# Rotary halves copied by ScalarE, parameters copied earlier, and a first query product that waits tile by tile

## What is computed

```python
mod = adaln(c, w_mod[l], b_mod[l])[:, None, :]          # silu(cond) @ w_mod + b_mod
mod_c = adaln(c_ctx[None, :], w_mod[l], b_mod[l])[:, None, :]
h = modulate(rmsnorm(x, p['g_pre_mix']), sh1, sc1)       # 1024 tokens
h_c = modulate(rmsnorm(ctx, p['g_pre_mix']), sh1c, sc1c) # 256 context tokens
...
def apply_rope(x, cos, sin):
    half = DIFF_HEAD // 2                                # 32
    x1, x2 = x[..., :half], x[..., half:]
    return jnp.concatenate([x1 * cos - x2 * sin, x1 * sin + x2 * cos], axis=-1)
```

## Time and profile before

| | |
|---|---|
| time, median of 3 runs | 3546.27 us (3546.17 to 3559.31) |
| time of the profiled execution | 3547.34 us |
| its span | 3545.4 us |
| mean granted TensorE clock | 0.977 |
| TensorE busy (matmul) | 3366.9 us, 95% |
| VectorE busy | 1923.6 us, 54% |
| ScalarE busy | 907.9 us, 26% |
| opening, until the first query product | 0 to 58.5 us |
| heads, until the last copy | 58.5 to 268 us |

### The profile page before, as it was taken

One profiled execution on the slowest core, in us unless ns is written; L12 is line 12 of the kernel. 1 busy time (PEld: TensorE's weight loads), 2 busy tenths in 40 slices (PEclk: granted clock), 3 DMA queues, 4 the chain that ended last, 5 costly groups with the idle time before them and its releaser, 6 DMA issues.

```text
span 3545.4 us, 57659 instructions
## 1 busy us (share of the span) xinstructions
PE 3366.9 (95%) x25645; PEld 2093.7 (59%) x25645; DVE 1923.6 (54%) x3171; ACT 907.9 (26%) x1850; POOL 51.2 (1%) x117
## 2 busy tenths in 40 slices
PE   6998879998999999889999999999999999999998
PEld 3445655558888888444444444445566447777753
DVE  2036763537676676655555550126988775444524
ACT  3005651115454554221010000100111413233310
POOL 2000000000000000000000000000000000000000
PEclk9999999999999999999999999999999999999999
DMA  6001002310000000331111112113011121100021
GB/s 242 0 0 56 1 24 72 120 58 3 18 18 4 4 4 17 115 113 65 48 59 48 45 60 80 43 59 98 24 36 36 62 76 54 36 24 24 1 89 65
DMA packets 110715, 177.24 MB, mean 50 GB/s; under 512 B 5443, under 2 KB 66626, under 8 KB 109826
## 3 DMA queue, kind: packets, MB, share of 16 engines
q1 hardware_dynamic: 101682, 144.67, 12.1%
q10 hardware_dynamic: 8784, 28.89, 2.3%
HBM read 147.33 MB, written 26.21 MB: 49 GB/s over the span
## 4 chain that ended last, share of the span: by engine, by line
PE 83%; DVE 9%; ACT 4%; DMA 2%; issue 1%; POOL 0%; ACTq 0%; DVEq 0%; SPq 0%; POOLq 0%
PE psum_all L66 82%; ACT sbuf_all L72 3%; DVE sbuf_all L91 3%; DVE sbuf_all L99 2%; DVE sbuf_all L81 2%; PE psum_all L111 1%; ACT L72 1%; DMA sbuf_all<-in_x 1%; DVE sbuf_all L105 1%; DVE sbuf_all L88 0%; DMA sbuf_all<-in_w_out 0%; DMA sbuf_all<-in_w_up 0%; DVE sbuf_all L111 0%; POOL sbuf_all L81 0%; DMA yd_spill<-sbuf_all 0%
## 5 line engine op out<-in xcount | busy, mean ns | idle before, releaser
L66 PE MATMUL psum_all<-sbuf_all 64*64 64x64 f32 (+8 forms) x24890 | 3270.0, 318 | 135.0 <-ACT sbuf_all L72 60.7
L66 PEld LDWEIGHTS psum_all<-sbuf_all 64*64 64x64 f32 (+3 forms) x24890 | 2010.7, 155 | 1370.7 <-issue 980.2
L72 ACT ACTIVATE sbuf_all<-psum_all 128x256 f32<-128x256 f32 (+6 forms) x889 | 363.9, 427 | 1457.6 <-PE psum_all L66 1316.7
L91 DVE SCALAR_TENSOR_TENSOR sbuf_all<-sbuf_all 128x520 f32<-128x520 f32 (+8 forms) x783 | 581.0, 776 | 16.9
L81 DVE TENSOR_TENSOR sbuf_all<-sbuf_all 128x640 f32<-128x640 f32 (+11 forms) x543 | 450.6, 853 | 134.2 <-ACT sbuf_all L72 91.3
L72 ACT ACTIVATE sbuf_all<-sbuf_all 128x64 f32<-128x64 f32 (+12 forms) x475 | 266.5, 574 | 821.5 <-DVE sbuf_all L75 349.1
L75 DVE COPY sbuf_all<-psum_all 128x256 f32<-128x256 f32 (+6 forms) x141 | 72.5, 524 | 473.4 <-PE psum_all L66 448.3
L72 ACT ACTIVATE sbuf_all<-psum_all,sbuf_all 128x1280 f32<-128x1280 f32 (+5 forms) x212 | 164.4, 781 | 313.5 <-PE psum_all L66 275.2
L81 DVE TENSOR_TENSOR sbuf_all<-sbuf_all,psum_all 128x512 f32<-128x512 f32 (+2 forms) x160 | 102.0, 639 | 250.6 <-PE psum_all L66 249.3
L105 DVE COPY_PREDICATED sbuf_all<-sbuf_all,psum_all 128x256 f32<-128x256 int32 (+2 forms) x296 | 144.0, 490 | 69.7 <-PE psum_all L66 64.1
L87 DVE TENSOR_SCALAR sbuf_all<-sbuf_all 128x256 f32<-128x256 f32 (+9 forms) x151 | 57.4, 417 | 162.6 <-ACT sbuf_all L72 159.4
(11 more groups left out here) (21 smaller groups left out, 167.6 us busy)
## 6 DMA issues: line engine op xcount, KB each, us to landing
sbuf_all<-in_w_mod SPq DMA_DIRECT2D x12, 2048.0 KB, 7.9
sbuf_all<-in_w_up SPq DMA_DIRECT2D x22, 1024.0 KB, 7.6
sbuf_all<-in_w_in SPq DMA_DIRECT2D x6, 2048.0 KB, 9.5
x_spill<-sbuf_all SPq DMA_DIRECT2D x16, 512.0 KB, 2.8
sbuf_all<-in_conv_w_in SPq DMA_DIRECT2D x16, 512.0 KB, 5.2
sbuf_all<-in_gla_w_in SPq DMA_DIRECT2D x8, 1024.0 KB, 5.3
sbuf_all<-in_w_down SPq DMA_DIRECT2D x4, 1792.0 KB, 7.5
hid_spill<-sbuf_all ACTq DMA_DIRECT2D x9, 512.0 KB, 2.6
```

Of the source, the lines that this page charges most:

```text
L66: return self.e.matmul(out, lhsT, rhs, start=start, stop=stop, skip_group_check=True)
L72: return self.e.activation(out, in_, func, bias=bias, scale=scale, **kw)
L91: return self.e.scalar_tensor_tensor(out, a, s, b, op0, op1) if self.e is not None else Unissued()
```

## The change

Three edits. The halves of the rotary embedding are swapped by ScalarE: for each half piece four activations of 32 partitions x 512 columns, two of them with scale -1, from the piece into `K.rot` at partitions shifted by 32; the 16 matmuls, their PSUM banks and the matrix `turn` go, and VectorE reads `K.rot` where it read PSUM. VectorE and ScalarE now work on the first four pieces during the key products and on the other four during the value products. The transposes and copies of parameter groups 1 to 6 stand ahead of modulation block 3 on TensorE and VectorE. And the first norm does the token columns of each tile before its context columns, while TensorE waits for one tile at a time in its query products and for the whole of the first norm only ahead of the key products.

```diff
@@ opening_scalar, and the same in opening_vector
-        for a, b, scale, shift in ((0, CTX, K.gs1c, K.modc), (CTX, ALL, K.gs1, K.mod)):
+        for a, b, scale, shift in ((CTX, ALL, K.gs1, K.mod), (0, CTX, K.gs1c, K.modc)):
             x = K.hT[:, j, a:b]
-            se.activation(x, x, ACT.Identity, ...).then_inc(*O.s.tick())
+            se.activation(x, x, ACT.Identity, ...).then_inc(*O.s.tick("first_norm", j, a))
@@ opening_vector
     turned(2)
+    for g in range(1, len(K.groups)):
+        params(g)
     modulation(3)
     mod_turned(3)
...
-    for g in range(1, len(K.groups)):
-        params(g)
@@ heads_tensor
-    te.wait_ge(*K.opening.v.by("first_norm"))
-    te.wait_ge(*K.opening.s.final())
     te.wait_ge(*K.opening.g.final())
+    def rows(k, a, b):
+        te.wait_ge(*(K.opening.s if k % 2 else K.opening.v).by("first_norm", k, CTX))
+        return hT[:, k, CTX + a:CTX + b]
     w = open_block(K, te, ("q",), 512)
...
-            product(te, bank, lambda k: w[:, k, j * P:(j + 1) * P], lambda k: hT[:, k, CTX + a:CTX + b],
+            product(te, bank, lambda k: w[:, k, j * P:(j + 1) * P], lambda k: rows(k, a, b),
                     KD).then_inc(*H.t.tick("q", j, s))
     K.weights.end(("q",), H.t.now())
+    for e in (K.opening.v, K.opening.s):
+        te.wait_ge(*e.final())
     w = open_block(K, te, ("k",), 512)
...
-        if i == 0:
-            te.wait_ge(*H.s.by("qk"))
-            te.wait_ge(*H.v.by("qk"))
-            te.wait_ge(*K.dma("rope").final())
-        if i < len(ROPES):
-            for half in range(2):
-                x, _, _ = rope_views(K, i, half)
-                bank = open_bank(K, te, "rope", i, half)
-                te.matmul(bank, K.turn, x).then_inc(*H.t.tick("rope", i, half))
@@ heads_scalar
+    def turned(n):
+        for half in range(2):
+            x, rot, _ = rope_views(K, n, half)
+            if n >= 4:
+                se.wait_ge(*H.v.by("k", n - 4))
+            se.wait_ge(*H.s.by("qk", n))
+            if n:
+                se.wait_ge(*H.v.by("rope", n - 1, half))
+            for at in range(0, P, 64):
+                se.activation(rot[at:at + 32, :], x[at + 32:at + 64, :], ACT.Copy, scale=-1.0).then_inc(*H.s.tick())
+                se.activation(rot[at + 32:at + 64, :], x[at:at + 32, :], ACT.Copy).then_inc(*H.s.tick("rope", n, half))
     for j in range(4):
         a, b = SPANS[1]
         se.wait_ge(*H.t.by("k", j, 1))
         ...
+        turned(j)
     for i in range(10):
         se.wait_ge(*H.t.by("v", i))
         ...
+        if i < 4:
+            turned(4 + i)
@@ heads_vector
+    def rope(n):
+        ve.wait_ge(*K.dma("rope").final())
+        for half in range(2):
+            x, rot, cols = rope_views(K, n, half)
+            ve.wait_ge(*H.s.by("rope", n, half))
+            ve.tt(rot, rot, K.sin[:, cols], ALU.mult).then_inc(*H.v.tick())
+            ve.tt(x, x, K.cos[:, cols], ALU.mult).then_inc(*H.v.tick())
+            ve.wait_ge(*H.v.now())
+            ve.tt(x, x, rot, ALU.add).then_inc(*H.v.tick("rope", n, half))
     for j in range(4):
         for s in (0, 2):
             ...
-    for n in range(len(ROPES)):
-        ... (the same three operations, the first one from PSUM)
+        rope(j)
+    for j in range(4):
+        rope(4 + j)
```

More of the change, by code:

```diff
@@ L416, in opening_scalar @@
         se.wait_ge(*O.s.by("turned", j))
-        for a, b, scale, shift in ((0, CTX, K.gs1c, K.modc), (CTX, ALL, K.gs1, K.mod)):
+        for a, b, scale, shift in ((CTX, ALL, K.gs1, K.mod), (0, CTX, K.gs1c, K.modc)):
             x = K.hT[:, j, a:b]
-            se.activation(x, x, ACT.Identity, scale=scale[:, j:j + 1], bias=shift[:, j:j + 1]).then_inc(*O.s.tick())
+            se.activation(x, x, ACT.Identity, scale=scale[:, j:j + 1], bias=shift[:, j:j + 1]).then_inc(*O.s.tick("first_norm", j, a))
 def opening_vector(K, ve):
@@ L494, in opening_vector @@
     for j in range(0, KD, 2):
-        for a, b, scale, shift in ((0, CTX, K.gs1c, K.modc), (CTX, ALL, K.gs1, K.mod)):
+        for a, b, scale, shift in ((CTX, ALL, K.gs1, K.mod), (0, CTX, K.gs1c, K.modc)):
             x = K.hT[:, j, a:b]
-            ve.ts(x, x, scale[:, j:j + 1], ALU.mult, shift[:, j:j + 1], ALU.add).then_inc(*V.tick("first_norm"))
-    for g in range(1, len(K.groups)):
-        params(g)
+            ve.ts(x, x, scale[:, j:j + 1], ALU.mult, shift[:, j:j + 1], ALU.add).then_inc(*V.tick("first_norm", j, a))
 def opening_tensor(K, te):
@@ L575, in attention_memory @@
     at = sb.at
-    K.cos, K.sin, K.turn = sb.take(SEQ), sb.take(SEQ), sb.take(P)
+    K.cos, K.sin = sb.take(SEQ), sb.take(SEQ)
     K.rot = [sb.take(BANK), sb.take(BANK)]
@@ L637, in heads_scalar @@
         se.wait_ge(*s)
-    for name, to in (("rope_cos", K.cos), ("rope_sin", K.sin), ("rope_turn", K.turn)):
+    for name, to in (("rope_cos", K.cos), ("rope_sin", K.sin)):
         se.dma_start(to, K.io[name]).then_inc(*K.dma("rope").tick())
+    def turned(n):
[9 more added lines that the diff above has]
+                se.activation(rot[at + 32:at + 64, :], x[at:at + 32, :], ACT.Copy).then_inc(*H.s.tick("rope", n, half))
     for j in range(4):
@@ L648, in heads_scalar @@
         se.wait_ge(*H.t.by("k", j, 1))
-        se.activation(K.k[:, j, a:b], K.bank.view("k", j, 1), ACT.Copy).then_inc(*H.s.tick("qk"))
+        se.activation(K.k[:, j, a:b], K.bank.view("k", j, 1), ACT.Copy).then_inc(*H.s.tick("qk", 4 + j))
         K.bank.end(("k", j, 1), H.s.now())
+        turned(j)
     for i in range(10):
@@ L664, in heads_vector @@
             ve.wait_ge(*H.t.by("k", j, s))
-            ve.copy(K.k[:, j, a:b], K.bank.view("k", j, s)[:, 0:b - a]).then_inc(*H.v.tick("qk"))
+            ve.copy(K.k[:, j, a:b], K.bank.view("k", j, s)[:, 0:b - a]).then_inc(*H.v.tick("k", j))
             K.bank.end(("k", j, s), H.v.now())
-    ve.wait_ge(*K.dma("rope").final())
-    ve.wait_ge(*H.s.by("qk"))
-    for n in range(len(ROPES)):
[L670 to L678, removed]
+        rope(j)
+    for j in range(4):
+        rope(4 + j)
 def heads_sync(K, sy):
@@ L3711, in rope_tables @@
     ang = np.concatenate([row[:, None] * inv, col[:, None] * inv], axis=-1)
[L3712 to L3717, removed]
     tile = lambda t: np.ascontiguousarray(np.tile(t.T, (4, 1)).astype(np.float32))
-    return {"rope_cos": tile(np.cos(ang)), "rope_sin": tile(np.sin(ang)), "rope_turn": turn}
+    return {"rope_cos": tile(np.cos(ang)), "rope_sin": tile(np.sin(ang))}
 def kernel(**inputs):
```

2 lines of the change are left out of this document (1 added, 1 removed).

## The result

| | before | after |
|---|---|---|
| median | 3546.27 us (13 runs, 3534.16 to 3559.31) | 3521.13 us (13 runs, 3513.87 to 3527.70) |
| ratio | | 0.9933, 95% interval 0.992 to 0.9946 |
| profiled execution, span | 3545.4 us | 3522.8 us |
| matmul records | 25645 | 25613 |
| ScalarE busy | 907.9 us | 947.3 us |

The kernel is 0.67% faster, about 24 us. The forecast was 19.2 us and 3527.1 us; the range of 3521 to 3534 just holds the measured 3521.13.

What follows compares the result with a forecast made beforehand. TensorE, filling 95% of the span, was taken as the bound. 13.75 us from the rotary matmuls plus 5.4 us from the earlier query start made 19.2 us: 3546.27 to 3527.1 us, range 3521 to 3534.

Steps and rivals of the forecast that it cites:

- the row of the same length: Profile row of a 128 x 512 SBUF-to-SBUF activation, taken as the cost of each rotary copy in the heads: 0.63 us.
- the rival of late parameters: Before modulation block 3, TensorE waits up to 3.6 us for parameters; part of a lost-gain rival, chance 0.20.
- my two rows: Two earlier low-clock stretches on TensorE, where the clock rose 3.8 and 5.0 us after it started.
- All later stages should shift as they are: Behind the heads stage, later stages keep their lengths and end 19 us sooner.
- the price of a low clock stretch in a later stage: In later stages, one low clock stretch costs 1.7 to 2.5 us; two fewer would help by 4 us.
- the rival of the run with the matmuls put back: Extra 4 to 6 us came from a lucky scan start; giving back 13.75 us costs 18 to 20; no chance given.

Runs made afterwards that it cites:

- edit 2 alone: Kernel before with only the parameter transposes and copies moved ahead of modulation block 3; ratio 1.000 to before.
- the best version: Changed kernel with parameters back behind the first norm and two unused filler matmuls before the queries; ratios to before 0.9936, then 0.9947.
- the parameters back: Changed kernel with the parameter transposes and copies back behind modulation block 3 and the first norm; ratio 0.9944 to before.
- double copies: Changed kernel with one extra copy into unused memory for each of ScalarE's 64 rotary copies; ratio 0.9937 to before.
- the idle time filled: Changed kernel with four unused 128 x 256 matmuls in TensorE's idle times ahead of the first query product; ratio 0.9934 to before.
- the matmuls put back: Changed kernel with 16 unused matmuls of the old size at their old places, ScalarE still making the rotary copies; ratio 0.9983 to before.
- three copies: Changed kernel with two extra copies into unused memory for each of ScalarE's 64 rotary copies; ratio 0.9976 to before.
- edits 2 and 3: Kernel before with the parameters moved and the first norm tile by tile, the rotary matmuls kept; ratio 0.9986 to before.

## Why the prediction was right, point by point

**Edit 1** was forecast at 13.75 us and gave 13.75. The copies cost 0.65 us each, where 0.63 was taken from the row of the same length; the shift by 32 partitions costs nothing that shows. The estimate of 0.72 us by the Trainium skill's page "ScalarE: Activation LUTs", Rules for kernel authors, is above what is measured here; the 0.3 us in it is stated for an activation with a bias per partition, which these copies don't have. They are hidden, as said, and with much in hand: twice as many are hidden too.

**Edit 2** was forecast as a loss of 0.8 us and is one of 0.63. VectorE's copies stayed under block 3, and the rival of late parameters did not come about: TensorE did not wait there.

**Edit 3** was forecast at 5.4 us together with the loss of edit 2, and first query copies come 5.89 us sooner: 5.11 from the earlier start and 0.78 from a shorter low clock (8.84 instead of 9.62 us from first matmul to copy). The clock did fall again, but only 0.7 us after TensorE had started (54.53), and it rose at 57.94: 4.1 us behind the start, between the 3.8 and 5.0 of my two rows, of which 3.4 us were low. That low time, taken as half lost, accounts for the 0.78: (5.0 - 3.4) / 2. (Of the 2.75 us between 9.62 and 6.87, which the prediction put down to the clock, this working explains 2.5; about 0.25 us from the last matmul to the copy is there at any clock, 9.62 - 2.5 and 8.84 - 1.7 being 7.1 us both times.)

**The sum** of these was 19.2 us and came out as 19.6. That the wait at 58.50 us was ScalarE's and not VectorE's, against what the chain of waits names, was read from the code and is shown by edit 2 alone.

**What was off** is the sentence "All later stages should shift as they are". They do in the program, not in an execution. Over the fourteen profiles, project and scan together take 885.3 to 895.2 us and the softmax 259.9 to 265.0, while the stretch from the first feed-forward product to the conformer's long products takes 942.6 to 943.5. One program differs by itself: the two profiles of the best version have 893.13 and 889.13 us for project and scan, 264.41 and 262.59 for the softmax. Two profiles of the changed kernel in which the clock changed at nearly the same moments (54.53 and 54.72 us) have the same softmax, 262.46 and 262.50 us, and the same project and scan, 889.70 and 889.69; a third (54.16 us) has 259.93 and 888.51. The term that was sized wrong is the price of a low clock stretch in a later stage. I had put it at 1.7 to 2.5 us, and two of them as the most that could help; in the scan one costs up to 7.8 us (23.27 less 15.49). So the range was too narrow on that side. That the median still lies in it, by 0.13 us, is luck, and so is part of the nearness of the total to the forecast.

**What stays open** is the mean. Over all occasions before has a mean of 3544.3 us (82 runs) and the changed kernel one of 3521.0 (25 runs), 23.3 us apart with a 95% interval of about 2.3, which leaves out the 19.6 of the stages. By occasions it was 26.2, 25.6 and 18.7 us. If an edit carried the extra 3.7 us, the other kernels with that edit should show it. Taking from each total mean the distance to its last value copy leaves 3324.5 us before; 3318.5 for the rotary edit alone, 3320.8 for the changed kernel, 3321.9 with the parameters back, 3323.4 with double copies and 3324.5 with the idle time filled, 3324.8 for the best version, 3324.1 with the matmuls put back, 3325.2 with three copies, but also 3320.5 for edit 2 alone and 3323.4 for edits 2 and 3. That is no pattern by edit, with standard errors of 0.7 to 2 us each.

The spread within one kernel goes with the clock. For 69 runs of the kernel before the mean granted clock is on record too: their times fall as it rises (correlation -0.93), by 2.7 us for each 0.001. But the means of the clock, 0.9769 before and 0.9782 in the changed kernel, explain little of the 3.7 us. By my estimate 0.0010 of that difference is the shorter low stretch at the first product (53.25 to 63.49 us before, 54.53 to 57.94 after), which the 19.6 us hold already; the other 0.0003 would be 1 us. The spreads say more about where the rest sits: the fastest runs are 20.3 us apart (3534.16 and 3513.87), but 12 of the 82 runs of before take over 3555 us, 21 us above its fastest, while none of the 25 of the changed kernel, nor of the 81 of the other kernels (5 to 12 of each), lies more than 18.2 us above the fastest of its own kernel. Why only the kernel before has such runs is not shown; that the moment at which the scan begins decides it, the rival of the run with the matmuls put back, is not excluded.

## What to carry to other kernels

Work that TensorE does only to move data between partitions can go to an engine with time to spare: here 2.6 us of ScalarE (four copies) replaced each 0.86 us of TensorE, and that was a gain because the one was hidden and the other was not. A wait on several engines should be checked against the code: the engine that the profile names need not be the one that counts. Where repeated runs spread by 25 us, judge a change of 20 us by the stage it touches, counted from a row ahead of it, and use the totals only to see that nothing else moved.

## What the runs showed of the hardware

The granted clock changed at other moments in three profiles of one program: it fell at 54.53, 54.16 and 54.72 us and rose again at 57.94, 57.57 and 58.13. In a stage of many small matmuls it also falls while TensorE is busy all the time (kernel before, from 910 to 955 us: 44.99 of 45.00 us busy, at a clock of 0.81):

```profile
910.00:955.00 45.00, 44.99 (x961) 0.81 0.01 3
```

There it weighs as much as the edits here: 491 records in 21.96 or 29.7 us, and 25 us between the fastest and slowest run of the kernel before (3534.16 and 3559.31). The Trainium skill's page "TensorE: Matmul & The Clock Gate", Part 1, says that the moment of the rise varies from run to run, and the three rises above agree. The same part puts the cost of the rise at the start below 1% of a typical kernel; here the clock falls again and again, and its mean of 0.977 means that 2.3% of the full clock was not granted, idle time included.

An activation of 32 x 512 whose output starts 32 partitions away from its input takes 0.629 us, as long as one of 128 x 512 from SBUF to SBUF in the kernel before (0.632 us, x32). Back to back the shifted ones follow each other every 0.65 us (eight in 5.21).

```profile
L72 ACT ACTIVATE sbuf_all<-sbuf_all 32x512 f32<-32x512 f32 x64 | 40.3, 629 | 1.6
```
